# The adaLN products of a two-layer trunk: from VectorE and GpSimd to column strips on TensorE

## The chip, the cores and the metric

The kernel runs on one core of a Trainium2 chip. The metric is the device time of one execution in microseconds (us), lower is better. TensorE does the matrix products, VectorE, ScalarE and GpSimd work on tiles, and SyncE (SP) issues the loads. In the rows of the profile they are PE (with PEld for its weight loads), DVE, ACT, POOL and SP.

## The reference, cut to what matters

Two layers run over 512 tokens of width 1024. Each begins with an adaLN modulation: the conditioning vector `c` goes through SiLU and is multiplied by a 1024 x 6144 matrix, `w_ada`. The result is six vectors of 1024 (shift, scale and gate for each of two sub-layers).

```python
ada = jax.nn.silu(c) @ w_ada[l] + b_ada[l]      # 1 x 1024 times 1024 x 6144
# sub-layer 1: h = rms(x) * g_norm_mix * (1 + scale) + shift
# then w_in; branches GLA, DSA and RWKV-7; merge; w_out; gated residual
# sub-layer 2: the PEER mixer, with its own shift, scale and gate
```

The matrix is 24 MiB in fp32 for a layer and is read once. The product is a matrix with one vector, 6144 sums of 1024 terms. Shift and scale of sub-layer 1 (part 0 below) are needed before anything of the layer can be projected; the other parts are needed later.

## The kernel before, in words

Everything is fp32, and activations lie transposed: 128 partitions are 128 channels, `KD` = 8 tiles of channels by 512 tokens. Each engine has one instruction stream, written out in program order, and the streams meet on semaphores. Eight PSUM banks are handed out in the fixed order of `layer_banks()`: entry n takes bank n modulo 8 and waits until the entry eight places earlier has been read (`opened` on TensorE).

**Loads.** SyncE issues them in the order of `BLOCKS`, into a ring of two slots (`ring`; semaphores `landed`, `used`). The first three blocks, `("ada", 0..2)`, are 1024 x 512 pieces of `w_ada` of 2 MiB each. The other nine pieces come as 18 half blocks of 1024 x 256 (1 MiB) into two buffers `a_half`, between the blocks `rw` 1, 0 and 2 as `ADA_AFTER` says. Half block n waits for `ada_used[n % 2]`, so for the use of half block n - 2; SyncE issues in order, so a block behind a waiting half block waits too.

**The adaLN product.** In a loaded piece, partition p of tile k holds row 128 k + p of `w_ada`, and `cond[:, k]` holds SiLU(c) for the same rows. VectorE's `lane_sums` (L1251, L1254) multiplies tile k by the column `cond[:, k]` and adds the eight tiles up, lane by lane. VectorE does so for the three full blocks and for half blocks 0, 1, 3 and 17; GpSimd does it for the other 14 (L1731 multiplies all eight tiles, L1734 and L1736 add them in pairs). The result `a_at[block]` is 128 x 512: what is left is the sum over partitions. `adaln(part)` on TensorE (L468) takes it, with each 128 x 128 piece as the stationary side and a column of ones moving: 16 products of one column for each of three parts. `modulation(part)` on VectorE (L1277) adds the bias.

**The stage around it.** TensorE: sum of squares (L456), `adaln(0)`, then, once the normalized input `hT` is there, block `rw` 3 (tiles rp 12 and 13, L484), the products z and za (L496, L499), blocks `rw` 1 and `rw` 0 (four tiles each, L484), `adaln(1)`, the first tile of `rw` 2, the products kkn and bon (four each, L456), the other three tiles of `rw` 2, `adaln(2)`; then the RWKV steps (from L536). Each projected tile goes PSUM to ScalarE (L963) to VectorE, which mixes it with its shifted copy (L1309, L1311). After the fourth tile of `rw` 1, VectorE has a long piece of scans and elementwise products (L1347 to L1365). ScalarE then squares for kkn (L981), and VectorE makes the factors for bon (L1317). Before RWKV, VectorE needs the last tile (L1309, L1311) and four products with bon (L1371).

Of the kernel before, what the change touches and what calls it, by code (L numbers as in the profile page):

```python
# [20 lines left out]
P = 128  # L21
# [47 lines left out]
ADA_LENT = (3, 17)  # L69
# [45 lines left out]
def layer_banks():  # L115

    o = [("ss", 0), ("mod", 0)]
    o += [("rp", c) for c in (12, 13)] + [("z", c) for c in range(4)] + [("za", c) for c in range(4)]
    o += [("rp", c) for c in (4, 5, 6, 7, 0, 1, 2, 3)] + [("mod", 1), ("rp", 8)]
    o += [("kkn", c) for c in range(4)] + [("bon", c) for c in range(4)] + [("rp", c) for c in (9, 10, 11)] + [("mod", 2)]  # L120
# [35 lines left out]
def trunk(nc, fixed, cols, consts, x_t, w_ada, w_in, w_small, w_uq, w_iq, w_mac, w_mb, w_out, w_pq, uv, out,  # L156
          depth=L):
    ctx = ExitStack()
    with ctx:
# [19 lines left out]
        cond = sb("cond", KD)  # L179
        modc = sb("modc", 48)  # L180
# [128 lines left out]
        class Sig:  # L309
# [8 lines left out]
            ("squares", 1 + KD), ("h_ready", 2 * KD), ("cond_ready", 1), ("ada_summed", 6), ("ada_half_summed", ADA_HALVES - 4),  # L318
# [23 lines left out]
        const_set = sem("const_set")  # L342
        rstd_ready = sem("rstd_ready")
# [90 lines left out]
        def _(pe):  # L434
# [26 lines left out]
            for l in range(0, depth):  # L461
                def adaln(part):

                    ps = opened(("mod", part), l)
                    for j in range(16):
                        if part == 0 and j % 4 == 0:
                            need("ada_summed", l, j // 4 + 1)
                        last = mm(ps[:, 16 * part + j:16 * part + j + 1], a_at[4 * part + j // 4][:, j % 4 * P:(j % 4 + 1) * P], ones[:, 0:1],  # L468
                                  start=True, stop=True)
                    pe.drain().then_inc(B.filled(("mod", part)), 1)  # L470

                need("squares", l, 1)
                summed(("ss", 0), l, [(ones, hT[:, k, :]) for k in range(KD)])
                adaln(0)
# [3 lines left out]
                def block_of(name, l, jobs, width):  # L478

                    w = v3(arrive(name, l)[:, 0:8 * width], 8)  # L480
                    for i, (job, j, m) in enumerate(jobs):
# [1349 lines left out]
```

## Time and profile before

| | us |
|---|---|
| median of 3 runs | 5007.51 (5005.51 to 5007.78) |
| the profiled execution, its own time | 5002.27 |
| its span in the profile | 5000.5 |
| from the start to the first RWKV product, layer 0 | 231.56 |
| from the start of layer 1 (2494) to its first RWKV product (2711.25) | 217 |

The times are those of whole executions; every duration below is of the one profiled execution. "Span" is the time from its first to its last instruction, 1.8 us less than its own time. The two layers run the same program; the stage that the change touches lies at the start of each.

### The profile page before, as it was taken

The page shows a single profiled execution, that of the slowest core. Times are in us where ns is not written, and L with a number is a line of the kernel's source. Part 1 is how long each engine was busy: PE and PEld are TensorE (multiplying, and loading weights), DVE is VectorE, ACT ScalarE, POOL GpSimd, SP SyncE. Part 2 cuts the span into 40 slices and gives each one's busy share as a digit, 9 for nine tenths or more (in the row PEclk, how much of TensorE's full clock was granted, in tenths as well). Part 3 has the DMA queues.
Part 4 walks back from the last instruction along what each step waited for, and adds up shares of the span by engine and source line. Part 5 has one row for each costly group of instructions (what it writes and reads, how often), then busy time and mean ns, then how long its engine had stood idle before and what let it go on. Part 6 is the DMA issues. An engine that isn't in the chain of part 4 may idle for free.

```text
span 5000.5 us, 46222 instructions
## 1 busy us (share of the span) xinstructions
PE 4085.7 (82%) x12452; PEld 1976.0 (40%) x12452; DVE 2612.1 (52%) x5380; ACT 1478.2 (30%) x4170; POOL 2093.2 (42%) x2276
## 2 busy tenths in 40 slices
PE   5699999996777777787777999999877777877776
PEld 2387444553333233232234864454532332322222
DVE  6843235147656656654467422351566566566444
ACT  2121231213333333333312122221233333333333
POOL 4622000005666656666555210000066666666664
PEclk8899999998999899999978999999999989999999
DMA  6300111128999999999952001111299999999997
GB/s 225 109 1 1 43 63 64 59 74 345 404 386 393 388 391 392 392 402 415 385 198 76 1 1 56 56 59 59 101 372 404 381 397 383 397 401 387 403 409 316
DMA packets 223813, 1223.86 MB, mean 245 GB/s; under 512 B 18240, under 2 KB 59840, under 8 KB 89024
## 3 DMA queue, kind: packets, MB, share of 16 engines
q0 software_dynamic: 147456, 1073.81, 53.5%
q1 hardware_dynamic: 76096, 147.10, 8.4%
q8 instruction: 99, 1.62, 0.1%
q14 instruction: 162, 1.33, 0.1%
HBM read 1218.74 MB, written 2.10 MB: 244 GB/s over the span
## 4 chain that ended last, share of the span: by engine, by line
PE 25%; POOL 21%; issue 19%; DVE 13%; DMA 9%; PEld 5%; ACT 3%; DVEq 2%; PEldq 2%; POOLq 1%; ACTq 0%; SPq 0%
POOL reg L1777 14%; DMA reg<-uv,e_ic 7%; POOL e_ic L1774 7%; PE bank L888 4%; PE bank L567 3%; PE bank L456 3%; PEld bank L456 3%; PE bank L821 2%; PE bank L558 2%; DVE reg L1677 2%; DVE reg L1590 2%; DVE reg L1585 2%; PEld bank L749 1%; PE bank L649 1%; PE bank L630 1%
## 5 line engine op out<-in xcount | busy, mean ns | idle before, releaser
L888 PE MATMUL bank<-reg,hT 128*128 128x512 f32 x4096 | 2022.5, 637 | 616.7 <-ACT hT L1195 616.2
L1677 DVE CUSTOM_DVE_ANT_0 reg<-reg 128x1024 f32<-128x1024 f32 x1024 | 1256.4, 1227 | 1041.1 <-DMA reg<-uv,e_ic 963.7
L1777 POOL DMA_INDIRECT reg<-uv,e_ic x1024 | 1202.4, 1174 | 852.7 <-POOL e_ic L1774 757.8
L888 PEld LDWEIGHTS bank<-reg,hT 128*128 128x128 f32 x4096 | 773.0, 200 | 1863.6 <-ACT hT L1195 1103.8
L1774 POOL COPY e_ic<-e_idx 128x1 uint32<-128x1 uint32 x1024 | 496.3, 485 | 1462.6 <-DVEq L1655 1282.4
L1189 ACT ACTIVATE reg<-reg 128x1 f32<-128x1 f32 x1024 | 207.3, 202 | 1501.4 <-DVEq L1678 1501.4
L456 PE MATMUL bank<-hT,reg 128*128 128x512 f32 x1120 | 497.3, 598 | 8.2 <-issue 6.3
L1195 ACT ACTIVATE hT<-con,reg 128x128 f32<-128x128 f32 x1024 | 411.1, 401 | 72.3 <-issue 2.3
L456 PEld LDWEIGHTS bank<-hT,reg 128*128 128x128 f32 x1120 | 211.8, 191 | 283.6 <-issue 283.6
L1191 ACT ACTIVATE reg<-reg 128x1 f32<-128x1 f32 x1024 | 301.5, 294 | 71.7 <-issue 1.7
L1755 POOL TENSOR_TENSOR reg<-reg,con 128x512 f32<-128x512 f32 x112 | 140.8, 1270 | 392.7 <-ACTq L1014 223.1
L1528 DVE TENSOR_TENSOR reg<-bank,reg 128x512 f32<-128x512 f32 x48 | 33.2, 692 | 372.3 <-PE bank L749 216.6
L567 PE MATMUL bank<-reg 128*128 128x128 f32 x1408 | 179.8, 282 | 14.8 <-ACTq L1014 14.1
L567 PEld LDWEIGHTS bank<-reg 128*128 128x128 f32 x1408 | 164.8, 193 | 27.5 <-ACTq L1014 22.5
L749 PE MATMUL bank<-reg 128*128 128x512 f32 x384 | 172.6, 592 | 0.0
L484 PE MATMUL bank<-hT,reg 128*128 128x512 f32 x320 | 145.6, 617 | 24.0 <-ACT hT L955 23.5
L1731 POOL TENSOR_TENSOR reg<-reg,cond 128x2048 f32<-128x2048 f32 x28 | 107.0, 3821 | 137.8 <-DMA reg<-w_ada 129.9
L1114 ACT ACTIVATE reg<-bank 128x512 f32<-128x512 f32 x48 | 28.7, 597 | 458.6 <-PE bank L456 458.6
L558 PE MATMUL bank<-reg 128*128 128x128 f32 x768 | 110.4, 292 | 19.6 <-issue 16.6
L1734 POOL TENSOR_TENSOR reg<-reg 128x1024 f32<-128x1024 f32 (+1 forms) x56 | 116.8, 2085 | 15.2 <-issue 7.3
L1407 DVE TENSOR_TENSOR reg<-bank,reg 128x512 f32<-128x512 f32 x80 | 55.3, 691 | 124.7 <-PE bank L567 119.4
L1590 DVE FIND_INDEX8 reg<-reg 128x8 uint32<-128x128 f32 (+1 forms) x384 | 118.2, 329 | 0.0
(257 smaller groups left out, 3748.5 us busy)
## 6 DMA issues: line engine op xcount, KB each, us to landing
reg<-w_ada SPq DMA_DIRECT2D x36, 1024.0 KB, 5.2
reg<-w_mac SPq DMA_DIRECT2D x16, 1536.0 KB, 6.4
reg<-w_in SPq DMA_DIRECT2D x10, 2048.0 KB, 8.0
reg<-uv,e_ic POOLq DMA_INDIRECT x1024, 8.6
reg<-w_ada SPq DMA_DIRECT2D x6, 2048.0 KB, 12.1
reg<-w_mb SPq DMA_DIRECT2D x8, 1536.0 KB, 6.5
reg<-w_out SPq DMA_DIRECT2D x4, 2048.0 KB, 7.8
reg<-w_pq SPq DMA_DIRECT2D x4, 2048.0 KB, 7.8
```

The source lines that it names most:

```text
L456: last = mm(ps[:, 0:n], a, b, start=(i == 0), stop=(i == len(parts) - 1))
L558: last = mm(ps[:, i * P:(i + 1) * P], r_m[lv % 2][:, h, :], r_tn[:, h, :], start=True, stop=True)
L567: last = mm(ps[:, i * P:(i + 1) * P], a_[:, h, :], b_[:, h, :], start=True, stop=True)
L749: last = mm(ps[:, :], w[:, i, 8 + k, :], y[:, k, :], start=(k == 0), stop=(k == 3))
L888: last = mm(acc[j][:, :], e_diag[:, s_, :], e_row[s_][:, D + j * NB:D + (j + 1) * NB], start=False, stop=False)
L1189: A(e_ge[:, s_:s_ + 1], e_dot[:, s_:s_ + 1], ACT.Gelu)
L1191: A(e_wg[:, s_:s_ + 1], e_gc[:, s_:s_ + 1], ACT.Copy, scale=e_ge[:, s_:s_ + 1])
L1195: A(e_diag[:, s_, :], ident, ACT.Copy, scale=e_wg[:, s_:s_ + 1]).then_inc(diags[s_], 1)
L1590: V.max_index(places[:, g, 8 * r:8 * r + 8], vals[:, g, 8 * r:8 * r + 8], src[:, g, :])
L1677: V.tensor_tensor_reduce(e_row[s_][:, 0:D], e_row[s_][:, 0:D], e_hc, 1.0, 0.0, ALU.mult, ALU.add, e_dot[:, s_:s_ + 1])
L1774: pool.tensor_copy(e_ic[:, s_:s_ + 1], e_idx[:, bass.ds(t * SLOTS + g * GRP + s_, 1)]).then_inc(idx_ready, 1)
L1777: pool.indirect_dma_start(e_row[s_], None, uv, bass.IndirectOffsetOnAxis(ap=e_ic[:, s_:s_ + 1], axis=0))\
```

## The change

The lane sums go. (In the diff the `adaln_part` with `A(...)` is ScalarE's, the lines with `lane_sums` and `half_block` are VectorE's, those with `nc.gpsimd` GpSimd's, the rest TensorE's.) A loaded piece becomes the moving side of products on TensorE, and the stationary side is the conditioning vector: VectorE once copies `cond[:, k]` into 32 columns for each k (`condb`, 128 x 8 x 32). The product for tile k writes 32 partitions of a bank, the strip 32 (k % 4); all 32 rows of a strip are equal. Tiles k and k + 4 add up in one strip, so a piece takes 8 products and leaves four strips of partial sums. There are 21 pieces in a layer, `adaln_part(0..20)`: three of 512 columns, 18 of 256. ScalarE copies each bank to `a_at`, and `adaln(part)` works as before, but its moving column is now `sc[:, 4:5]`, which is 1 in rows 0, 32, 64 and 96 and 0 elsewhere.

Pieces 0 to 4 stand between the sum of squares and `adaln(0)`, 5 and 6 after block `rw` 3, 7 after z, 8 after za, 9 to 16 one behind each tile of `rw` 1 and `rw` 0, 17 and 18 after the first tile of `rw` 2, 19 and 20 between kkn and bon. The banks' order gets 21 entries more, each piece waits for its bank, and each ends with a drain of TensorE. The order of the loads stays; what frees their buffers is now TensorE. GpSimd does nothing ahead of the RWKV steps.

```diff
+                    need("ad_copied", l, (5, 13, 21)[part])
                     for j in range(16):
-                        if part == 0 and j % 4 == 0:
-                            need("ada_summed", l, j // 4 + 1)
-                        last = mm(ps[:, 16 * part + j:16 * part + j + 1], a_at[4 * part + j // 4][:, j % 4 * P:(j % 4 + 1) * P], ones[:, 0:1],
+                        last = mm(ps[:, 16 * part + j:16 * part + j + 1], a_at[4 * part + j // 4][:, j % 4 * P:(j % 4 + 1) * P], sc[:, 4:5],
...
+                def adaln_part(i):
+                    ps = opened(("ad", i), l)
+                    if i < ADA_RING:
+                        w, n, freed = v3(arrive(("ada", i), l)[:, 0:4096], 8), 512, used[block_at(("ada", i))[1]]
+                    else:
+                        h = i - ADA_RING
+                        pe.wait_ge(ada_landed[h % 2], 16 * (l * (ADA_HALVES // 2) + h // 2 + 1))
+                        w, n, freed = a_half[h % 2], 256, ada_used[h % 2]
+                    for k in range(KD):
+                        q = 32 * (k % 4)
+                        last = mm(ps[q:q + 32, 0:n], condb[:, k, :], w[:, k, :], start=(k < 4), stop=(k >= 4))
+                    last.then_inc(freed, 1)
+                    pe.drain().then_inc(B.filled(("ad", i)), 1)
...
-                need("ada_half_summed", l, 7)
-                need("ada_summed", l, 5)
                 adaln(1)
...
+                def adaln_part(i):
+                    ps = full(("ad", i), l)
+                    if i < ADA_RING:
+                        A(a_at[i], ps[:, :], ACT.Copy).then_inc(B.freed(("ad", i)), 1)
+                    else:
+                        h = i - ADA_RING
+                        A(a_at[ADA_RING + h // 2][:, h % 2 * 256:(h % 2 + 1) * 256], ps[:, 0:256], ACT.Copy).then_inc(B.freed(("ad", i)), 1)
+                    act.drain().then_inc(G["ad_copied"].sem, 1)
...
-                for i in range(ADA_RING):
...
-                    lane_sums(a_at[i], v3(dst[:, 0:4096], 8))
...
-                half_block(0)
-                half_block(1)
...
-                half_block(ADA_LENT[0])
...
-                        half_block(ADA_LENT[1])
...
-                for n in range(2, ADA_HALVES):
-                    if n in ADA_LENT:
-                        continue
...
-                    nc.gpsimd.tensor_tensor(w, w, bc(cond[:].unsqueeze(2), [P, 8, 256]), ALU.mult)
-                    pool.drain()
-                    for m in (4, 2):
-                        nc.gpsimd.tensor_tensor(w[:, 0:m, :], w[:, 0:m, :], w[:, m:2 * m, :], ALU.add)
-                        pool.drain()
-                    nc.gpsimd.tensor_tensor(a_at[block_i][:, n % 2 * 256:(n % 2 + 1) * 256], w[:, 0, :], w[:, 1, :], ALU.add)
```

TensorE, from the start of a layer to the products z. Before, the sum of squares (L456), `adaln(0)` (L468), the two tiles of `rw` 3 (L484) and the first z (L496):

```order
L456 MATMUL bank0<-hT,con 128x512 x8
L468 MATMUL bank1<-con,reg 128x1 x16
L484 MATMUL bank2<-hT,reg 128x512 x8
L484 MATMUL bank3<-hT,reg 128x512 x8
L496 MATMUL bank4<-reg,sw 128x512
```

And of the changed kernel, where L476 is a piece (its output form is that of one strip), L485 is `adaln`, L504 a tile of `rw` and L520 z:

```order
L459 MATMUL bank0<-hT,con 128x512 x8
L476 MATMUL bank1<-reg,condb 32x512 x8
L476 MATMUL bank2<-reg,condb 32x512 x8
L476 MATMUL bank3<-reg,condb 32x512 x8
L476 MATMUL bank4<-reg,condb 32x256 x8
L476 MATMUL bank5<-reg,condb 32x256 x8
L485 MATMUL bank6<-sc,reg 128x1 x16
L504 MATMUL bank7<-hT,reg 128x512 x8
L504 MATMUL bank0<-hT,reg 128x512 x8
L476 MATMUL bank1<-reg,condb 32x256 x8
L476 MATMUL bank2<-reg,condb 32x256 x8
L520 MATMUL bank3<-reg,sw 128x512
```

Five pieces now stand in front of `adaln(0)`, and two between `rw` 3 and z.

TensorE, from the last tile of `rw` 0 to the first kkn. Before:

```order
L484 MATMUL bank2<-hT,reg 128x512 x8
L484 MATMUL bank3<-hT,reg 128x512 x8
L468 MATMUL bank4<-con,reg 128x1 x16
L456 MATMUL bank5<-hT,reg 128x512 x8
L456 MATMUL bank6<-reg,con 128x512
```

And of the changed kernel, the same place, where L459 is first the tile of `rw` 2 and then kkn:

```order
L504 MATMUL bank1<-hT,reg 128x512 x8
L476 MATMUL bank2<-reg,condb 32x256 x8
L504 MATMUL bank3<-hT,reg 128x512 x8
L476 MATMUL bank4<-reg,condb 32x256 x8
L485 MATMUL bank5<-sc,reg 128x1 x16
L459 MATMUL bank6<-hT,reg 128x512 x8
L476 MATMUL bank7<-reg,condb 32x256 x8
L476 MATMUL bank0<-reg,condb 32x256 x8
L459 MATMUL bank1<-reg,con 128x512
```

Behind each projected tile stands a piece, and two more stand in front of kkn.

## Rows read from the trace of the kernel before

**Rows 1.** By stretch: length, busy us (instructions) of each engine, granted clock, DMA share, GB/s.

```profile
0.00:231.56 231.56, 143.68 (x369) 71.47 (x369) 173.72 (x141) 45.58 (x62) 127.82 (x60) 0.83 0.53 180
2494.00:2711.25 217.25, 151.62 (x369) 73.36 (x369) 162.71 (x135) 44.39 (x60) 125.88 (x56) 0.77 0.50 169
```

**Rows 2.** Timeline, TensorE, layer 0: start, us, what, xcount [idle before <-releaser].

```profile
116.51 27.70 PE L484 MATMUL bank<-hT,reg 128*128 128x512 f32 x64 [0.26 <-issue]
144.57 4.24 PE L468 MATMUL bank<-con,reg 128*128 128x1 f32 x32 [0.35 <-issue]
149.04 9.75 PE L456 MATMUL bank<-hT,reg 128*128 128x512 f32 x16 [0.23 <-issue]
171.88 5.16 PE L456 MATMUL bank<-reg,con 128*128 128x512 f32 x8 [13.08 <-ACT reg L981]
188.28 5.49 PE L456 MATMUL bank<-reg,con 128*128 128x512 f32 x8 [11.25 <-DVEq L1319]
193.61 20.76 PE L456 MATMUL bank<-hT,reg 128*128 128x512 f32 x48
224.37 6.96 PE L468 MATMUL bank<-con,reg 128*128 128x1 f32 x32 [9.99 <-DVEq L1342]
```

**Rows 3.** Timeline, TensorE, layer 1, at kkn, bon and `adaln(2)`.

```profile
2655.15 5.97 PE L456 MATMUL bank<-reg,con 128*128 128x512 f32 x8 [14.55 <-ACT reg L981]
2671.55 6.30 PE L456 MATMUL bank<-reg,con 128*128 128x512 f32 x8 [10.43 <-DVEq L1319]
2704.06 6.96 PE L468 MATMUL bank<-con,reg 128*128 128x1 f32 x32 [5.60 <-DVEq L1342]
```

**Rows 4.** Timeline, layer 0: VectorE, and GpSimd's last instruction of the stage.

```profile
119.78 11.47 DVE L1347 TENSOR_TENSOR_SCAN reg<-con,reg 128x512 f32<-128x512 f32 x4
165.13 3.93 DVE L1311 SCALAR_TENSOR_TENSOR reg<-reg,col 128x512 f32<-128x512 f32 x1
...
210.70 0.75 DVE L1311 SCALAR_TENSOR_TENSOR reg<-reg,col 128x512 f32<-128x512 f32 x1
...
215.45 2.29 DVE L1338 TENSOR_TENSOR reg<-reg 128x2048 f32<-128x2048 f32 x1
...
201.79 0.99 POOL L1736 TENSOR_TENSOR reg<-reg 128x256 f32<-128x256 f32 x1
```

**Rows 5.** Timeline at both layers' starts; last, the page's row of 2 MiB loads.

```profile
17.26 9.09 PE L456 MATMUL bank<-hT,con 128*128 128x512 f32 x16 [17.26 <-ACT hT L948]
...
53.04 12.30 DVE L1292 SCALAR_TENSOR_TENSOR hT<-xT,gain,rstd 128x512 f32<-128x512 f32 x8
...
66.15 15.42 PE L484 MATMUL bank<-hT,reg 128*128 128x512 f32 x32 [13.77 <-ACT hT L955]
...
2498.33 9.31 PE L456 MATMUL bank<-hT,con 128*128 128x512 f32 x16 [6.59 <-ACT hT L948]
...
2535.22 5.39 DVE L1292 SCALAR_TENSOR_TENSOR hT<-xT,gain,rstd 128x512 f32<-128x512 f32 x8
...
2541.42 16.81 PE L484 MATMUL bank<-hT,reg 128*128 128x512 f32 x32 [9.71 <-ACT hT L955]
...
reg<-w_in SPq DMA_DIRECT2D x10, 2048.0 KB, 8.0
```

**Rows 6.** Timeline, TensorE, a step whose products write two strips of 64 partitions.

```profile
276.66 0.34 PE L608 MATMUL bank<-reg 128*64 128x64 f32 x4
276.83 0.29 PE L609 MATMUL bank<-reg 128*64 128x64 f32 x4
276.94 0.34 PE L608 MATMUL bank<-reg 128*64 128x64 f32 x4
277.06 0.33 PE L609 MATMUL bank<-reg 128*64 128x64 f32 x4
```

**Rows 7.** By stretch, as rows 1: behind `adaln(1)` of layer 0.

```profile
149.00:151.00 2.00, 1.96 (x3) 0.96 (x4) 2.00 (x1) 0.00 (x0) 1.89 (x1) 0.50 0.00 0
```

More of the change, by code:

```diff
@@ L115, in layer_banks @@
 def layer_banks():
[L117 to L120, printed above, removed]
+    o = [("ss", 0)] + [("ad", i) for i in range(5)] + [("mod", 0)]
+    o += [("rp", 12), ("rp", 13), ("ad", 5), ("ad", 6)] + [("z", c) for c in range(4)] + [("ad", 7)] + [("za", c) for c in range(4)] + [("ad", 8)]
+    o += [x for i in range(4) for x in (("rp", 4 + i), ("ad", 9 + i))] + [x for i in range(4) for x in (("rp", i), ("ad", 13 + i))]
+    o += [("mod", 1), ("rp", 8), ("ad", 17), ("ad", 18)]
+    o += [("kkn", c) for c in range(4)] + [("ad", 19), ("ad", 20)] + [("bon", c) for c in range(4)] + [("rp", c) for c in (9, 10, 11)] + [("mod", 2)]
     for half, t, q, stage in rwkv_steps():
@@ L317, in trunk @@
         G = {n: Sig(n, k) for n, k in (
[L318 removed]
+            ("squares", 1 + KD), ("h_ready", 2 * KD), ("ad_copied", ADA_PARTS),
             ("pt_ready", 14), ("pt_used", 14), ("mixed", 14), ("lr_ready", 2), ("sig_ready", 2),
@@ L473, in _, with block_of @@
                 summed(("ss", 0), l, [(ones, hT[:, k, :]) for k in range(KD)])
+                pe.wait_ge(cond_spread, 1)
+                for i in range(5):
+                    adaln_part(i)
                 adaln(0)
                 need("h_ready", l, KD)
-                def block_of(name, l, jobs, width):
+                def block_of(name, l, jobs, width, parts=None):
                     w = v3(arrive(name, l)[:, 0:8 * width], 8)
@@ L951, in norm @@
                     inv_roots([(rstd[:], ("ss", w))], 1.0 / D, sc[:, 0:1], rstd_ready)
+                    if w == 0:
+                        for i in range(5):
+                            adaln_part(i)
                     for k in range(KD):
@@ L1241, in _ @@
             dve.wait_ge(loaded, 64)
+            V.tensor_tensor(sc[:, 4:5], ident[:, 0:1], ident[:, 32:33], ALU.add)
+            V.tensor_tensor(sc[:, 5:6], ident[:, 64:65], ident[:, 96:97], ALU.add)
+            dve.drain()
+            V.tensor_tensor(sc[:, 4:5], sc[:, 4:5], sc[:, 5:6], ALU.add)
+            dve.wait_ge(cond_ready, 1)
+            V.tensor_copy(condb, bc(cond[:].unsqueeze(2), [P, KD, 32]))
+            dve.drain().then_inc(cond_spread, 1)
             for l in range(0, depth):
@@ L1366, in _ @@
                         dve.drain()
-                need("ada_half_summed", l, ADA_HALVES - 5)
+                for i in range(2):
+                    dve.wait_ge(ada_used[i], (l + 1) * (ADA_HALVES // 2) + 1)
+                dve.sem_inc(passed, 1)
                 for c in range(4):
```

60 lines of the change are left out of this document (25 added, 35 removed).

## The prediction

> **What bounds the kernel now.** I first asked for each stretch how busy the engines were, then for the timeline of TensorE in the stage that the change touches. From the start to the first RWKV product TensorE works 143.7 of 231.6 us, and in layer 1 151.6 of 217 [rows 1]; VectorE is busier, 173.7 and 162.7. The rest of the span, 4550 us, does not run one changed instruction, so whatever happens comes from some 450 us. The timeline shows where TensorE stood still: 13.1 us ahead of kkn until ScalarE's square, 11.3 us ahead of bon, 10.0 us ahead of `adaln(2)` [rows 2], and the same three in layer 1, 14.6, 10.4 and 5.6 us [rows 3]. All end with something that VectorE made or set off. The reader is to see next why VectorE was late. The same instruction on the same form, L1311, took 3.93 us at 165.13 and 0.75 us at 210.70. GpSimd's last lane sum of the layer ended at 202.8, and behind it every VectorE instruction is at its short duration, 2.29 us for four times the size [rows 4]. So VectorE is slow while GpSimd runs its sums: the eight norm products of a layer took 12.3 us in layer 0, with GpSimd at work, and 5.4 us in layer 1, without [rows 5]. The last of the three stalls is another thing: VectorE's own sum of half block 17.
>
> **What goes.** VectorE's seven lane sums and GpSimd's 14 go in each layer. The long piece behind the fourth tile of `rw` 1 began at 119.78 and let the next tile be mixed some 40 us later. Its four scans took 11.47 us [rows 4]; undisturbed I estimate the piece at 18 to 22 us, from 2.29 us for each of its three products of 2048 columns and the shortest forms of the rest. VectorE would then be through at about 140, while TensorE is still projecting tiles until about 150. kkn waits for the first tile of `rw` 2 only, bon for nothing, and `adaln(2)` for no lane sum. I take away all three stalls in both layers: 13.1 + 11.3 + 10.0 + 14.6 + 10.4 + 5.6 = **65 us**. What is late next is TensorE itself.
>
> **Clock.** TensorE's granted clock was 0.50 (1.2 GHz) in the stretch behind the 32 one-column products of `adaln(1)` [rows 7], and it is low behind each stall. At full clock one of the two passes of a 512-column product takes 27.70 / 64 = 0.433 us [rows 2]. kkn and bon have 8 passes each, 3.6 us with the tail; they took 5.16, 5.49, 5.97 and 6.30, so **8.5 us** are to be had if no stall stands before them. `adaln(2)` took 6.96 us after its stall and 4.24 where the clock was still up [rows 2, 3]: **5.4 us** in two layers. Parts of the start of layer 1 ran slow after short waits that the pieces now fill; I put 3 us.
>
> **What is added on TensorE.** No row shows strips of 32. Upper bound for a piece of 256 columns: its 8 products in 16 passes run one after another, 16 x 0.217 = 3.5 us and the edges. Lower bound: four strips run at once, 4 x 0.217 = 0.87 us. The nearest row is the step that writes two strips of 64: 16 passes of 64 columns within 0.73 us of 276.66, the last one starting some 0.5 us after the first [rows 6]. Streaming alone would ask 0.433 / 8 = 0.054 us each, 0.87 us in sequence. And the second group of L608 is under way before the first L609 group is finished, though it stands behind it in the program. So strips do run beside one another, with two passes of each product waiting in their strip. I take the lower bound with edges: 0.26 us at the drain [rows 2] and about 0.16 us for the last pass to finish, 0.87 + 0.42 = **1.3 us**. A piece of 512 columns is 2.2 us at full clock, 3.9 at half.
>
> Part 3, section "The mechanism", of the page "TensorE: Matmul & The Clock Gate" of the Trainium skill says otherwise: products start and end strictly in program order, and a weight load overlaps a running product only in another row group. By that rule a strip's second pass would hold up the next strip, and the third rival below is what it gives. The L608 rows of this trace speak against it.
>
> From block `rw` 3 to RWKV 16 pieces stand on TensorE's path in each layer: 32 x 1.3 = **41.6 us**. Nothing hides them now that TensorE is the late one. Two small things more. Piece 7 needs half block 4, which is issued when piece 5 is done; between lie only piece 6 and z, about 4.7 us, and a half block takes 5 to 6, so 0.8 us a layer. And RWKV now waits for VectorE's last tile and bon products, about 5 us behind the last tile of `rw` 2, a little longer than `adaln(2)` covers: 0.8 a layer. Together **3.2 us**. ScalarE gets 21 copies of at most 0.6 us a layer; it is busy 45 of 231 us [rows 1], and only the last ones before `adaln(0)` stand on the path.
>
> **The start of a layer.** Before, lane sums ran beside the sum of squares. Now piece 0 waits for the end of that sum, 26.3 [rows 5], and frees its ring slot at 28.4, so block 2 is issued 4 us later. A 2 MiB load takes 8.0 us [rows 5]: it is there at 36.4. TensorE has been idle, so I put half clock: piece 2 to 40.3, pieces 3 and 4 to 44.7, the copy to 45.3, `adaln(0)` 5.6 us (between 4.24 and 6.96) to 50.9, the gain to 51.5. From there to `rw` 3 layer 1 took 6.2 us (2535.22 to 2541.42): 57.7 instead of 66.15, **8.4 us** less. Layer 1 by the same steps: 2507.6, 2509.8, 2517.8, 2521.7, 2526.1, 2532.3, then 0.7 to 2533.0, and 2539.2 instead of 2541.42, **2.2 us** less. That gain is mostly the norm products' 12.3 us in layer 0; the product itself ends no sooner.
>
> **Sum.** 65 + 8.5 + 5.4 + 3 + 8.4 + 2.2 = 92.5 us go, 41.6 + 3.2 = 44.8 come: 47.7 us less. The profiled execution would be 5002.3 - 47.7 = 4954.6; the median lay 5.2 above it, which gives 4960 (0.9902 of the time before). Following both layers' timelines step by step instead of adding terms I get 55 to 58 us, with some waits shrinking further; hence the lower end.
>
> **Rivals.**
> 1. *The strips overlap only in part* (reading four full-height strips at once may be slower than two). A piece then costs 1.7 to 2.0 us: 32 x 0.4 to 0.7 = 13 to 22 us, and 3 to 5 at the starts. Time 4976 to 4987. Nothing excludes it, since only two strips were ever seen.
> 2. *The clock stays down.* Behind the one-column products of `adaln(1)` the granted clock was 0.50 [rows 7] and the next tile took 9.75 us instead of 6.9 [rows 2], 2.9 us. Were that so behind each of the 13 places with pieces, 13 x 2.9 x 2 = 75 us come: -48 + 75 = 27 slower, 5035. It turns slower once more than 8 of the 13 places cost this. Against it: the pieces are short, and between most of them stand 6.9 us of full products.
> 3. *Strict order.* Each product's second pass waits for the first, and the next strip starts beside the second: 9 x 0.217 + 0.42 = 2.4 us a piece, 32 x 1.1 = 35 us; the starts lose 2.2 us at piece 0, 4.3 at piece 2, 4.3 at 3 and 4, 22 us in two layers. Time 4960 + 57 = 5017, at the edge of slower.
> 4. *No overlap at all.* 3.9 us a piece, 83 us more, and some 50 at the starts: about 5095.
> 5. *VectorE is not freed.* If GpSimd is not what slows it, only the 10.0 and 5.6 us stalls and its own sums go, and the pieces cost 41.6: about 5020. Against it: all of VectorE's rows before and after 202.8.
>
> **How the numbers follow.** The forecast has 0.66, rival 1 0.12, rival 2 0.07, rival 3 0.08, rival 4 0.04, rival 5 0.03. The bounds of the forecast itself are 4938 (the step-by-step reading, pieces of 1.2 us, higher clock) and 4975. To hold 8 in 10 the range takes in rival 1 and its tail: 4936 to 4998. A measurement of this kernel tells 0.2% from no change, 10 us. Faster by more: 0.66 + 0.12 + a part of rival 3, 0.80. Within: half of rivals 3 and 5, 0.08. Slower: rivals 2 and 4 and the rest, 0.12.
>
> **What would show it.** The pieces' line: a piece of 256 columns within 1.2 to 1.4 us, its 16 passes overlapping in time; 3.5 us would be rival 4, 2.0 us with each strip beginning at the second pass of the one before rival 3. VectorE's L1311 at 0.75 us throughout the stage, the long piece at 18 to 22 us. No stall of TensorE over 2 us between `rw` 1 and RWKV. The first RWKV product at about 205 instead of 231.6. Granted clock 1.00 between the tiles of `rw` 1 and `rw` 0. It is wrong if TensorE waits for half blocks (each wait ending with a load of `w_ada`), or if the RWKV steps or the PEER part, where nothing changes, move by more than 2 us.

## The result

The changed kernel took 4953.32 us (median of 4 runs, 4950.52 to 4969.54) against 5006.83 us for the kernel before (4 runs, 5005.51 to 5007.78): a ratio of **0.9911, interval 0.9893 to 0.9929**. It is faster, by 53.5 us; the forecast was 4960. The profiled execution took 4950.52, with a span of 4948.7 where the kernel before had 5000.5.

The stretches first (length; busy us and instructions of PE, PEld, DVE, ACT, POOL; granted clock; DMA share; GB/s): the stage of layer 0, what follows it up to layer 1, the stage of layer 1, and the rest. The first and third answer to [rows 1].

```profile
0.00:209.35 209.35, 167.41 (x705) 75.26 (x705) 61.82 (x89) 54.57 (x83) 0.20 (x4) 0.93 0.58 197
209.35:2471.60 2262.25, 1893.59 (x5850) 915.75 (x5850) 1135.35 (x2549) 689.98 (x2019) 921.45 (x1080) 0.95 0.64 253
2471.60:2663.86 192.26, 164.52 (x704) 73.98 (x705) 60.89 (x79) 52.99 (x81) 0.00 (x0) 0.92 0.55 188
2663.86:4948.70 2284.84, 1907.27 (x5866) 924.55 (x5866) 1140.49 (x2556) 698.37 (x2030) 920.12 (x1080) 0.94 0.63 251
```

The stage shrank from 231.56 to 209.35 and from 217.25 to 192.26 us, together **47.2 us**. The stretches behind were 2262.4 and 2289.2 us long in the kernel before and are 2262.3 and 2284.8 now; the 4.6 us there are scatter of the part behind, where nothing changed: its PEER mixer, from the first to the last gather of a layer, took 1355 to 1368 us over all the runs below. VectorE's busy time in the stage fell from 173.7 to 61.8 us, GpSimd's from 127.8 to 0.2, and TensorE's rose from 143.7 to 167.4.

TensorE in layer 0, timeline (start, us, what, xcount, [idle before <-releaser]), to be laid beside [rows 2]:

```profile
37.01 3.64 PE L476 MATMUL bank<-reg,condb 128*32 128x512 f32 x16 [6.26 <-DMA reg<-w_ada]
40.92 1.36 PE L476 MATMUL bank<-reg,condb 128*32 128x256 f32 x16 [0.28 <-issue]
44.31 3.70 PE L485 MATMUL bank<-sc,reg 128*128 128x1 f32 x32 [0.67 <-ACTq L976]
54.88 15.85 PE L504 MATMUL bank<-hT,reg 128*128 128x512 f32 x32 [6.87 <-ACT hT L992]
...
99.45 1.07 PE L476 MATMUL bank<-reg,condb 128*32 128x256 f32 x16
...
107.71 1.07 PE L476 MATMUL bank<-reg,condb 128*32 128x256 f32 x16
...
168.06 3.67 PE L459 MATMUL bank<-reg,con 128*128 128x512 f32 x8 [0.28 <-issue]
175.29 1.94 PE L476 MATMUL bank<-reg,condb 128*32 128x256 f32 x16 [2.36 <-DMA reg<-w_ada]
177.50 5.66 PE L459 MATMUL bank<-reg,con 128*128 128x512 f32 x8 [0.28 <-issue]
...
204.03 3.70 PE L485 MATMUL bank<-sc,reg 128*128 128x1 f32 x32 [0.26 <-issue]
209.35 3.47 PE L562 MATMUL bank<-reg 64*128 64x256 f32 x16 [1.62 <-DVE reg L1396]
```

A piece of 256 columns is 1.07 us. Two pieces between tiles start 8.26 us apart (99.45, 107.71), where the tiles of [rows 2] came every 27.70 / 4 = 6.93: a piece costs 1.33 us in place. kkn waits 0.28 us where it waited 13.08, `adaln(2)` 0.26 where it waited 9.99. Ahead of bon one wait is left, of another kind: piece 20 waits 2.36 us for half block 17, and with TensorE at rest the clock falls. The granted clock in three stretches there (pieces 17 and 18 for comparison, piece 20, bon; columns as above):

```profile
165.30:168.00 2.70, 2.18 (x33) 0.92 (x32) 1.44 (x2) 1.10 (x3) 0.00 (x0) 1.00 0.13 24
175.30:177.50 2.20, 1.92 (x16) 0.67 (x17) 1.68 (x3) 1.15 (x4) 0.00 (x0) 0.50 1.05 394
177.50:183.00 5.50, 5.50 (x8) 2.39 (x9) 0.00 (x0) 2.22 (x3) 0.00 (x0) 0.63 0.40 146
```

At 1.00 (2.4 GHz) a piece is 1.07 us and kkn 3.67; behind the wait, at 0.50 (1.2 GHz), the piece is 1.94, and bon 5.66. The wait cost 2.4 + 0.9 + 2.0 us in this execution, not 2.4. Layer 1 has the same (piece 20 stayed at full clock there), answering to [rows 3]:

```profile
2631.00 1.07 PE L476 MATMUL bank<-reg,condb 128*32 128x256 f32 x16 [2.54 <-DMA reg<-w_ada]
2632.35 5.33 PE L459 MATMUL bank<-reg,con 128*128 128x512 f32 x8 [0.28 <-issue]
2658.54 3.70 PE L485 MATMUL bank<-sc,reg 128*128 128x1 f32 x32 [0.26 <-issue]
```

VectorE, layer 0, its long piece (first and last rows), and all 28 instructions of the mixing line in one row (ns, min/median/max), answering to [rows 4]:

```profile
118.45 4.57 DVE L1368 TENSOR_TENSOR_SCAN reg<-con,reg 128x512 f32<-128x512 f32 x4
...
131.82 2.29 DVE L1386 TENSOR_TENSOR reg<-reg 128x2048 f32<-128x2048 f32 x1
```

```profile
L1335 DVE SCALAR_TENSOR_TENSOR reg<-reg,col x28: 750/752/753, 65.3 to 2659.8; 128x512 f32<-128x512 f32 x28
```

The scans take 4.57 us instead of 11.47, the long piece 15.7 us instead of 39.8, and no mixing instruction is above 753 ns. In the kernel before the same row reads:

```profile
L1311 DVE SCALAR_TENSOR_TENSOR reg<-reg,col x28: 751/1596/4026, 76.4 to 2704.8; 128x512 f32<-128x512 f32 x28
```

### The profile page after: what moved, and what is told of

Its sections match the earlier page's. It is cut to its first block, busy times and chain, and to the rows that moved or that the text cites. A ratio compares the mean times of both kernels' runs of the same rounds, so it can differ in the third digit from the quotient of the medians.

```text
span 4948.7 us, 47208 instructions
## 1 busy us (share of the span) xinstructions
PE 4132.8 (84%) x13124; PEld 1989.5 (40%) x13124; DVE 2398.6 (48%) x5272; ACT 1495.9 (30%) x4212; POOL 1841.8 (37%) x2164
## 4 chain that ended last, share of the span: by engine, by line
PE 31%; POOL 22%; issue 19%; DVE 9%; DMA 8%; PEld 4%; ACT 3%; DVEq 1%; PEldq 1%; POOLq 1%; ACTq 0%; SPq 0%
POOL reg L1781 15%; DMA reg<-uv,e_ic 7%; POOL e_ic L1778 7%; PE bank L914 5%; PE bank L459 5%; PE bank L593 3%; PE bank L504 3%; PEld bank L459 3%; PE bank L847 2%; PE bank L584 2%; DVE reg L1700 2%; DVE reg L1613 2%; PEld bank L775 1%; DVE reg L1608 1%; PE bank L675 1%
## 5 line engine op out<-in xcount | busy, mean ns | idle before, releaser
L459 PE MATMUL bank<-hT,reg 128*128 128x512 f32 x1120 | 497.1, 598 | 8.2 <-issue 6.2
L459 PEld LDWEIGHTS bank<-hT,reg 128*128 128x128 f32 x1120 | 211.9, 191 | 283.4 <-issue 283.4
L775 PE MATMUL bank<-reg 128*128 128x512 f32 x384 | 172.6, 592 | 0.0
L1159 ACT ACTIVATE reg<-bank 128x512 f32<-128x512 f32 x48 | 28.7, 597 | 458.6 <-PE bank L459 458.6
L504 PE MATMUL bank<-hT,reg 128*128 128x512 f32 x320 | 145.7, 610 | 16.7 <-ACT hT L992 13.7
L847 PE MATMUL bank<-reg 128*128 128x512 f32 x256 | 112.3, 593 | 3.5 <-DVEq L1555 3.5
L1058 ACT ACTIVATE reg<-bank 128x512 f32<-128x512 f32 x96 | 57.3, 597 | 182.7 <-PE bank L584 182.7
```

The source lines that it names most:

```text
L459: last = mm(ps[:, 0:n], a, b, start=(i == 0), stop=(i == len(parts) - 1))
L504: last = mm(ps[0:m, :], w[:, k, j:j + m], hT[:, k, :], start=(k == 0), stop=(k == KD - 1))
L775: last = mm(ps[:, :], w[:, i, 8 + k, :], y[:, k, :], start=(k == 0), stop=(k == 3))
L847: last = mm(ps[:, :], w[:, k, j * P:(j + 1) * P], m_o[:, k, :], start=(k == 0), stop=(k == KD - 1))
```

## Experiments

Times are medians; "before" was run beside them each time (4998.81, 4997.64 and 4996.51 us on three occasions, single runs from 4980 to 5014). Since most of that scatter comes from the PEER part, lengths of the stage are read from the profile beside the times: "R0" is start to first RWKV product in layer 0, "R1" the same from the start of layer 1. The kernel before has R0 231.6 and R1 217.2, the changed kernel 209.3 and 192.3. Each run has a label (x10, x8, ...), given with its result.

### The changed kernel once more

> The changed kernel itself once more, beside the two kernels below on one chip. The first run of it gave a ratio of 0.9911 to the kernel before, with stage lengths of 209.3 us (start to the first RWKV product, layer 0) and 192.3 us (layer 1). Expected: 4950 us (4940 to 4965), the same stage lengths within 2 us.

x10: 4955.84 us (4949.46 to 4968.22, 5 runs), ratio 0.9924 (0.9906 to 0.9941). R0 210.2, but R1 198.5: in this execution the start of layer 1 ran at a lower clock (the products of `adaln(0)` took 6.06 us, not 3.70) and waited longer for block 2 and for half block 4. So one profiled layer can be off by 6 us. A difference of stages below that needs both layers, or more than one run, to speak for it. The wait for half block 17 is there again, 3.36 and 2.54 us, but in layer 1 the clock did not fall behind it, and bon took 3.67 us:

```profile
2647.38 1.07 PE L476 MATMUL bank<-reg,condb 128*32 128x256 f32 x16 [2.54 <-DMA reg<-w_ada]
2648.76 3.67 PE L459 MATMUL bank<-reg,con 128*128 128x512 f32 x8 [0.31 <-issue]
```

The same wait therefore costs 2.5 us in one execution and 5.3 in another.

### Why was VectorE late? GpSimd's sums taken away from the kernel before

Edit, in the kernel *before*:

```diff
-                    nc.gpsimd.tensor_tensor(w, w, bc(cond[:].unsqueeze(2), [P, 8, 256]), ALU.mult)
-                    pool.drain()
-                    for m in (4, 2):
-                        nc.gpsimd.tensor_tensor(w[:, 0:m, :], w[:, 0:m, :], w[:, m:2 * m, :], ALU.add)
-                        pool.drain()
```

> The kernel before, with GpSimd's large multiplications and the first two additions of each half block left out (14 half blocks a layer; the adaLN vectors are then wrong for those): only its last addition of 256 columns stays. All else, VectorE's own sums too, is as before. Theory: this is the gain without its price on TensorE. The stalls ahead of kkn and bon go (13.1 + 11.3 + 14.6 + 10.4 = 49 us), the norm products of layer 0 are 7 us shorter, the stall ahead of adaln(2) stays; 50 to 60 us less, profiled time 4945 (4938 to 4955). Rival (VectorE's own sums and waits, not GpSimd, made it late): less than 15 us, above 4987.

x8: 4911.49 us (3 runs), ratio 0.9828 (0.9811 to 0.9845); R0 190.1, R1 176.5, together 82 us shorter than before. VectorE kept all its own sums. TensorE and VectorE in layer 0:

```profile
150.94 7.03 PE L456 MATMUL bank<-reg,con 128*128 128x512 f32 x16
182.99 6.87 PE L468 MATMUL bank<-con,reg 128*128 128x1 f32 x32 [4.42 <-DVEq L1342]
...
112.72 4.57 DVE L1347 TENSOR_TENSOR_SCAN reg<-con,reg 128x512 f32<-128x512 f32 x4
```

kkn and bon run as one group of 16 without a stall, at full clock, and the scans are back at 4.57 us. Only VectorE's own half block 17 is still late. I had expected 50 to 60 us. The 82 are the 49 of the two stalls, 9 at the layers' starts (`rw` 3 begins 6.4 and 2.9 us earlier), 7 off the stall ahead of `adaln(2)` (9.99 to 4.42 us in layer 0, 5.60 to 4.56 in layer 1), and 17 of clock, for which I had put nothing: kkn and bon together 9 us shorter, and 8 behind the start of `rw` 3 in layer 1. Against the changed kernel this one is 19.2 and 15.8 us of stage shorter, although it keeps that last stall: roughly the price of the pieces.

How deep VectorE's slowdown is follows from what GpSimd has running. In the kernel before, GpSimd's large product stood beside the slow L1311 of [rows 4], which ran from 165.13 to 169.06:

```profile
164.86 3.65 POOL L1731 TENSOR_TENSOR reg<-reg,cond 128x2048 f32<-128x2048 f32 x1 [0.35 <-issue]
```

It ended at 168.51, and L1311 0.55 us later. All 22 slow instructions of that line, of both layers, end 0.55 us after the GpSimd instruction that was running when they began, whether they took 1.06, 1.60, 2.68 or 3.93 to 4.03 us; the six with no GpSimd instruction beside them take 0.75.

### GpSimd kept busy in the changed kernel

Edit, in the changed kernel's GpSimd stream (110 in the first, 85 in the second; the product is not used):

```diff
+                pool.wait_ge(*B.full(("mod", 0), l))
+                pool.sem_inc(passed, 1)
+                scratch = e_idx[:].bitcast(F32)
+                for _ in range(110):
+                    nc.gpsimd.tensor_tensor(scratch, con[:, 0:512], con[:, 512:1024], ALU.mult)
+                    pool.drain()
```

> The changed kernel, with work put back on GpSimd that nothing uses: 110 products of 512 columns from two constant areas into a scratch area, in each layer, from the first adaLN part to shortly before the RWKV steps. Theory (VectorE was slow because GpSimd worked beside it): VectorE's L1335 goes back from 0.75 us to between 1.6 and 4, its long piece behind the fourth tile from 15.7 us to 35 to 40, and TensorE waits ahead of bon again; 12 us a layer, profiled time about 4975 (4965 to 4985) instead of 4950.5. Rival (VectorE was relieved only of its own sums): VectorE's durations and the time stay, 4950.

x1: 5005.95 us (9 runs), ratio 1.0019 (1.0002 to 1.0036): the whole gain was gone, 31 us more than I expected. R0 227.4, R1 204.3. The trace shows why the time overstates it:

```profile
51.66 184.77 POOL L1746 TENSOR_TENSOR e_idx<-con 128x512 f32<-128x512 f32 x110 [51.21 <-PEq L487]
227.42 3.84 PE L562 MATMUL bank<-reg 64*128 64x256 f32 x16 [7.28 <-DVE reg L1396]
237.99 1.11 PE L576 MATMUL bank<-con,reg 128*128 128x128 f32 x4 [5.93 <-POOL reg L1765]
```

The dummy products came 1.68 us apart, gaps included; one of them took 1.54 on average. They ran 9 us into the RWKV steps, held up GpSimd's first real product there, and slowed the steps (from the first product to the last y product 265 and 276 us, not 258 and 256). So I ran it with fewer.

> x1 with 85 idle products of 512 columns on GpSimd per layer instead of 110, so that they end before the RWKV steps begin (85 x 1.68 = 143 us from about 52 us on ends near 195 us). Theory (GpSimd's work beside VectorE's slows VectorE alone; it is this that made the stalls together with the sums): VectorE's 512-column products of the tile mixes take 1.6 us again instead of 0.75, the long piece about 31 us instead of 15.7, the stage is 5 to 15 us longer than the changed kernel's, and the RWKV steps behind it are as long as in the changed kernel (255 us, not 264 to 275 as in x1). Time 4970 (4955 to 4985). Rival (GpSimd's work does not matter, x1's loss came from its dummy work running into the RWKV steps): the stage stays at 209 and 192 us.

x1b: 4963.15 us (one run). R0 218.5, R1 196.4; the RWKV steps are back at 256 us in both layers, so x1's excess there was its overrun. GpSimd and VectorE in layer 0, then the norm products of layer 1; below, the mixing line:

```profile
48.62 137.77 POOL L1746 TENSOR_TENSOR e_idx<-con 128x512 f32<-128x512 f32 x85 [48.16 <-PEq L487]
50.06 13.47 DVE L1318 SCALAR_TENSOR_TENSOR hT<-xT,gain,rstd 128x512 f32<-128x512 f32 x8
128.91 8.51 DVE L1368 TENSOR_TENSOR_SCAN reg<-con,reg 128x512 f32<-128x512 f32 x4
...
2517.45 5.39 DVE L1318 SCALAR_TENSOR_TENSOR hT<-xT,gain,rstd 128x512 f32<-128x512 f32 x8
2524.62 5.48 POOL L1746 TENSOR_TENSOR e_idx<-con 128x512 f32<-128x512 f32 x4 [7.35 <-issue]
```

```profile
L1335 DVE SCALAR_TENSOR_TENSOR reg<-reg,col x28: 751/1598/1619, 75.1 to 2673.0; 128x512 f32<-128x512 f32 x28
```

GpSimd busy makes VectorE slow: 1.60 us for 0.75, and 13.47 for the eight norm products that take 5.39. Layer 1 holds its own control: GpSimd paused for 7.35 us there (why, no row shows), and the norm products in the pause took 5.39. The slowing goes both ways: GpSimd's dummies took 1.29 us each while VectorE waited (84 to 100 us) and 1.91 beside its scans. In layer 0 the norm, on which TensorE waits, pays 8 us. Behind the first product of `rw` 3 the stage is no longer than in the changed kernel there (154.1 us against 154.5), although the long piece took 31 us. Layer 1 is 2.0 us longer behind `rw` 3 (153.5 against 151.5), with waits for VectorE that the changed kernel has not, or has shorter:

```profile
2640.54 1.07 PE L476 MATMUL bank<-reg,condb 128*32 128x256 f32 x16 [1.44 <-DVE modc L1303]
2677.12 3.49 PE L562 MATMUL bank<-reg 64*128 64x256 f32 x14 [3.92 <-DVE reg L1396]
```

In x1, where the dummies ran on to the end, the wait ahead of RWKV was 7.28 and 9.17 us instead of 1.62. So the norm and the last tile are the main places where a slow VectorE is paid for.

**Why, then, are there no stalls of 11 to 15 us?** Not because VectorE has no sums of its own any more. In the kernel before, its lane sums lie outside the stretch that mattered: half block 3 ended at 74.6, after which VectorE stood waiting for tiles, and the next sum began at 219.86. Between them stands VectorE's work up to the factors of bon (L1317; L1341 in the changed kernel), here first the kernel before, then x1b:

```profile
65.68 8.95 DVE L1254 SCALAR_TENSOR_TENSOR reg<-reg,cond 128x256 f32<-128x256 f32 x7
178.76 9.44 DVE L1317 SCALAR_TENSOR_TENSOR reg<-reg,col 128x512 f32<-128x512 f32 x4
...
173.65 6.57 DVE L1341 SCALAR_TENSOR_TENSOR reg<-reg,col 128x512 f32<-128x512 f32 x4
```

And x8, which keeps all of VectorE's sums, has no stall ahead of kkn or bon. What differs is, first, the depth of the slowdown: from the scans to the end of the factors VectorE needed 68.4 us in the kernel before (119.78 to 188.2), beside GpSimd instructions of up to 5.26 us, and 51.3 in x1b, beside dummies of 1.25. Second, TensorE comes later by itself: it reaches kkn 112.4 us after the start of `rw` 3 in x1b, since it now has the pieces to do, and would have reached it after 92.6 in the kernel before. Which of the two counts for more no run here separates.

### What does a piece cost, and how far do strips overlap?

One strip and two strips instead of four, same products (ScalarE's copies and `adaln` then read 32 and 64 partitions); and four strips with the second product of a strip right behind its first:

```diff
-                        q = 32 * (k % 4)
-                        last = mm(ps[q:q + 32, 0:n], condb[:, k, :], w[:, k, :], start=(k < 4), stop=(k >= 4))
+                        last = mm(ps[0:32, 0:n], condb[:, k, :], w[:, k, :], start=(k == 0), stop=(k == KD - 1))
...
-                        last = mm(ps[q:q + 32, 0:n], condb[:, k, :], w[:, k, :], start=(k < 4), stop=(k >= 4))
+                        q = 32 * (k % 2)
+                        last = mm(ps[q:q + 32, 0:n], condb[:, k, :], w[:, k, :], start=(k < 2), stop=(k >= 6))
...
-                    for k in range(KD):
+                    for k in (0, 4, 1, 5, 2, 6, 3, 7):
                         q = 32 * (k % 4)
```

> The changed kernel with all eight products of a piece in one strip of 32 partitions, so 16 passes one after another. Theory (four strips at once): a piece of 256 columns takes 16 x 0.217 + 0.16 = 3.6 us instead of 1.07, 32 x 2.5 = 81 us more between rw 3 and RWKV and 20 to 25 a layer at the starts, time about 5075 (5050 to 5100), so slower than the kernel before. Rival (the strips never ran at once, the pieces are short for another reason): the piece and the time stay, 1.07 us and 4950.

> The changed kernel with the eight products of a piece in two strips instead of four. Theory: the time of a piece is its passes per strip, 8 x 0.217 + 0.16 = 1.9 us instead of 1.07; 32 x 0.83 = 27 us more, about 7 a layer at the starts, time about 4991 (4980 to 5000). Rival (beyond two strips something shared, such as reading, is the limit): 1.07 to 1.3 us, within 8 us of 4950.

> The changed kernel with the products of a piece in the order k = 0, 4, 1, 5, 2, 6, 3, 7: the four passes of a strip stand one behind another in the program. Theory A (TensorE looks past any number of passes that wait for their strip): 1.07 us and 4950, as before. Theory B (it looks past about three waiting passes, as many as the z products waited for before za began in the trace of the kernel before): the strips start one after another, 1.5 to 2.2 us a piece, 4970 to 5000. Rival (products start strictly in program order): four strips in sequence, 3.6 us, about 5075.

A piece of 256 columns in the trace of one strip, of two, and of four in the other order:

```profile
104.00 3.64 PE L475 MATMUL bank<-reg,condb 128*32 128x256 f32 x16
```

```profile
107.50 1.92 PE L476 MATMUL bank<-reg,condb 128*32 128x256 f32 x16
```

```profile
94.06 1.09 PE L476 MATMUL bank<-reg,condb 128*32 128x256 f32 x16
```

The runs are x2 (one strip), x3 (two) and x4 (the other order).

| strips | piece, us | R0 / R1 | time |
|---|---|---|---|
| one | 3.64 | 258.6 / 243.2 | 5043.06 (one run) |
| two | 1.92 | 220.0 / 208.4 | 4981.41 (one run) |
| four, second product of a strip right behind | 1.09 | 210.3 / 193.4 | 4950.54 (one run) |
| four, as changed | 1.07 | 209.3 / 192.3 | 4953.32 |

Everything follows 16 x 0.217 us divided by the number of strips, plus 0.2. With one strip the change is a loss, 44 us over before in that session; with two it keeps a third of its gain. The stages of one strip are 49 and 51 us longer than of four: 15 at each start, and 34 and 36 behind it, a little below 16 x 2.57 = 41, since longer pieces leave the half blocks time to land. The time came out 32 us below the 5075 expected: I had put 122 us on the stages and 100 came, and the part between the two stages was 9 us short in that one run. The fourth kernel is the sharp one for the mechanism. Strictly in program order, the second product of strip 0 would hold up the first of strip 1, and each strip would begin with the last pass of the one before: 13 x 0.217, about 3 us a piece. The order costs 0.02 us. So a product waiting on its own strip does not hold up one for another strip.

### The waits that are left

Half blocks 16 and 17 are used one tile of `rw` 2 later; and at the start of a layer the pieces stand in the order 0, sum of squares, 1, 3, 4, 2 (half blocks 0 and 1 are there before block 2). ScalarE and the order of banks follow.

```diff
+                values(1)
                 adaln_part(19)
...
-                for j in range(1, 4):
+                for j in range(2, 4):
...
+                pe.wait_ge(cond_spread, 1)
+                adaln_part(0)
                 need("squares", l, 1)
                 summed(("ss", 0), l, [(ones, hT[:, k, :]) for k in range(KD)])
-                pe.wait_ge(cond_spread, 1)
-                for i in range(5):
+                for i in (1, 3, 4, 2):
                     adaln_part(i)
```

> The changed kernel with the second tile of rw 2 moved ahead of pieces 19 and 20, so that half block 17 has 6.9 us more to land. Theory: TensorE's wait of 2.4 us for it goes, and the clock stays up, so that piece 20 takes 1.07 us and not 1.94 and the bon products 3.7 and not 5.7: 4 to 5 us a layer, time 4942 (4938 to 4946). Rival (VectorE's last tiles then set the start of RWKV): under 2 us a layer, 4947 to 4951.

x5: 4952.28 us (4 runs), ratio 0.9901 (0.9879 to 0.9922); R0 209.1, R1 202.9. In layer 0 the wait for half block 17 is gone and bon is back at full clock, and a part of the gain is given back some twenty microseconds on:

```profile
183.05 3.67 PE L459 MATMUL bank<-reg,con 128*128 128x512 f32 x8 [0.28 <-issue]
209.06 3.92 PE L563 MATMUL bank<-reg 64*128 64x256 f32 x16 [3.73 <-DVE reg L1397]
```

RWKV now waits 3.73 us for VectorE, where it waited 1.62. From `rw` 3 to RWKV 3.2 us are won (151.2 against 154.5), and the start before it was 3.0 us longer in this execution, so R0 is the same. Layer 1 was 11 us longer in that execution, with 7.8 us of waits for half blocks elsewhere, which is near the scatter of x10. The 4 to 5 us a layer that I expected did not come; by itself this move shows nothing that I could measure.

> The changed kernel with the pieces at a layer's start in the order 0, sum of squares, 1, 3, 4, 2. Block 2 is issued some 7 us earlier and lands 2 to 3 us earlier, and pieces 3 and 4 (3 us) lie in the wait for it. Theory: adaln(0) comes 5 to 6 us a layer earlier, time 4940 (4936 to 4944). Rival (the loads are the limit there, block 2 lands when it did): the 3 us alone, 4945.

x6: 4948.22 us (4 runs), ratio 0.9899; R0 204.2, R1 187.5. The start of layer 0:

```profile
18.53 3.64 PE L476 MATMUL bank<-reg,condb 128*32 128x512 f32 x16 [18.53 <-DMA reg<-w_ada]
35.38 1.92 PE L476 MATMUL bank<-reg,condb 128*32 128x512 f32 x16 [1.25 <-DMA reg<-w_ada]
50.84 9.51 PE L505 MATMUL bank<-hT,reg 128*128 128x512 f32 x15 [6.87 <-ACT hT L995]
```

Piece 0 frees its slot 6 us earlier, and the wait for block 2 falls from 6.26 to 1.25 us. `rw` 3 begins at 50.84 instead of 54.88, and in layer 1 5.9 us earlier after its start. The stages are 5.1 and 4.8 us shorter, so both layers agree with the theory's 5 to 6 about as well as the scatter lets one see; the time, 4948, lies above both forecasts. Block 2 came 1.6 and 2.5 us earlier, although its slot was free 6 and 9 us earlier.

> Both of the changes of order together (pieces 19 and 20 behind the second tile of rw 2; at the start 0, sum of squares, 1, 3, 4, 2). Theory: they add up, 9 to 11 us a layer, time about 4931 (4926 to 4938). Rival (the earlier start only moves a wait for a half block): 4938 to 4945.

> The changed kernel with both moves of order (pieces 0, sum of squares, 1, 3, 4, 2 at a layer's start; half blocks 16 and 17 after the last receptance tile) once more. Its profile before gave stages shorter by 7.3 and 6.5 us than the changed kernel's. If that is real: 4938 us, 12 to 15 us below the repeat of the changed kernel on the same chip. If it was only one execution's scatter, the two come out equal.

(The edit of both is the same; what the second text calls the last receptance tile is the second tile of `rw` 2.) First (x7) 4942.04 us (5 runs), ratio 0.9893 (0.9876 to 0.9910), then (x11) 4938.03 (4 runs), ratio 0.9892 (0.9874 to 0.9910); R0 202.0 and 202.3, R1 185.8 and 185.5. The stages repeat within 0.3 us. In its second session it lay 17.8 us below the repeat of the changed kernel; the two ratios' intervals still overlap a little (0.9874 to 0.9910, and 0.9906 to 0.9941), so the stages, 7 us shorter in each layer, are the better evidence. The 9 to 11 us a layer that I first expected did not come: 7.3 and 6.5. RWKV now waits for VectorE, 2.60 and 3.72 us in x11.

### A split that uses what was learned

If GpSimd made the trouble and not VectorE's own work, VectorE can take a part of the sums back, and TensorE is rid of that many pieces. Half blocks 2 to 9 go to VectorE, in its idle time between the mixes; the rest is x11's.

```diff
+                def half_block(n):
+                    dve.wait_ge(ada_landed[n % 2], 16 * (l * (ADA_HALVES // 2) + n // 2 + 1))
...
+                    V.tensor_scalar(out_, w[:, 0, :], cond[:, 0:1], None, ALU.mult)
+                    for k in range(1, KD):
+                        dve.drain()
+                        V.scalar_tensor_tensor(out=out_, in0=w[:, k, :], scalar=cond[:, k:k + 1], in1=out_, op0=ALU.mult, op1=ALU.add)
+                    dve.drain().then_inc(ada_used[n % 2], 1)
...
+                half_block(2)
+                half_block(3)
...
+                    for n in {0: (4,), 1: (5, 6), 2: (7,), 3: (8,), 4: (9,)}.get(i, ()):
+                        half_block(n)
```

> x11 with half blocks 2 to 9 given back to VectorE, which multiplies and adds them all by itself in its idle time between the tile mixes (8 products of 256 columns per half block, nothing on GpSimd); adaLN part 1 then takes the column of ones again. TensorE keeps pieces 0 to 4 and 13 to 20. Theory (the 32 small pieces per layer are paid in full on TensorE at 1.35 us each, and what cost the kernel before its time was GpSimd's share, not VectorE's): eight pieces fewer give 8 x 1.35 = 10.8 us a layer, 21 to 22 us over x11, so about 4918 us; the distance of two tile ends in the first half falls from 8.27 to 6.9 us, VectorE's half block takes 8 x 0.45 = 3.6 us in an idle slot of 6.8 us. Rival (VectorE's work again comes late, or hinders others): TensorE waits for the tile mixes, and less than 10 us is won. If the half blocks go one after another into the slots, VectorE is never the late one before adaLN part 1.

x9: **4911.85 us** (4902.79 to 4929.84, 5 runs), ratio **0.9844 (0.9822 to 0.9867)**: faster than both kernels, and than x11 in the same session. R0 187.4, R1 175.7, 14.9 and 9.8 us below x11, 24.7 where 21 to 22 were expected. (The 32 pieces of the expectation are those of both layers.) TensorE and VectorE in layer 0:

```profile
71.21 27.73 PE L510 MATMUL bank<-hT,reg 128*128 128x512 f32 x64
187.40 3.92 PE L565 MATMUL bank<-reg 64*128 64x256 f32 x16 [3.72 <-DVE reg L1414]
...
87.69 0.35 DVE L1330 TENSOR_SCALAR reg<-reg,cond 128x256 f32<-128x256 f32 x1 [0.25 <-issue]
88.11 3.84 DVE L1333 SCALAR_TENSOR_TENSOR reg<-reg,cond 128x256 f32<-128x256 f32 x7
92.78 0.69 DVE L1349 TENSOR_TENSOR reg<-reg 128x512 f32<-128x512 f32 x1 [0.83 <-ACTq L1006]
```

The four tiles of `rw` 1 follow each other in 27.73 us again, as in [rows 2]. VectorE takes 4.3 us for a half block and is back 0.8 us before the next tile. What bounds the stage's end now is VectorE's last tile and bon products (3.72 us).

## Why the prediction was right, point by point

- **The stalls (65 us): right.** All three go in both layers, and what came next was TensorE itself, as said. The reason named first, GpSimd's sums slowing VectorE, is the cause by x8, which alone gets 82 us of stage. Rival 5 falls. Two corrections. "VectorE is slow while GpSimd runs" does not by itself say that TensorE waits: in x1b VectorE is slow too, less deeply, and beside a later TensorE, and the two stalls are not there. And the reading that `adaln(2)`'s stall was VectorE's own affair holds for most of it only in layer 1: in x8, where half block 17 is still VectorE's, the stall shrinks from 9.99 to 4.42 us in layer 0 and from 5.60 to 4.56 in layer 1.
- **A piece, 1.3 us: right**, 1.07 and the gap, 1.33 in place. The lower bound, not the two-strip row, was what held; two strips measured 1.92. The argument from [rows 6], that a waiting pass does not hold up another strip's, is borne out by x4. Rivals 1, 3 and 4 fall. The page "TensorE: Matmul & The Clock Gate" of the Trainium skill (Part 3, section "The mechanism") has products start strictly in program order. This case's fp32 products in strips do not (x4: 1.09 us a piece), and the measurement decides.
- **Clock (13.9 + 3 us): right for kkn** (3.67 in both layers) **and `adaln(2)`** (3.70; the 4.24 forecast was the row of `adaln(1)`), **wrong for bon**, 5.66 and 5.33 instead of 3.6. The step that failed is "bon for nothing": I had given piece 7 a wait for its half block and none to piece 20, which stands just as near behind the piece that frees its buffer. SyncE issues half blocks 16 and 17 when pieces 17 and 18 are done, and a load of 2 MiB of `w_in` right behind (SyncE's row, both half blocks; then the page's row of all half blocks, whose median to landing was 5.2 us before):

```profile
166.54 1.72 SPq L422 DMA_DIRECT2D reg<-w_ada  x2
reg<-w_ada SPq DMA_DIRECT2D x36, 1024.0 KB, 6.7
```

  Half block 17 was issued at 167.89 and had landed at 175.29, 7.4 us later, with the stretch around it at 394 GB/s. TensorE wanted it at 172.93: between pieces 18 and 20 stand only kkn and piece 19, 5.2 us. That wait cost 5.3 us in layer 0 and 2.5 + 1.7 in layer 1, some 9.5 us that the sum lacks (4.9 and 2.5 in x10). It is also what the prediction had named as a sign of being wrong, a wait for a half block, and it is over the 2 us that no stall was to exceed. **The 3 us for the start of layer 1 were mis-sized**: before, layer 1 took 58.5 us from the first product of `rw` 3 to the first of `rw` 0 and layer 0 50.4; now the two agree within 0.5. So 8 us of clock came back there, not 3. Piece 7 waited 0.45 us and not at all, less than the 0.8 given; RWKV's wait for VectorE was 1.62, twice the 0.8.
- **The start of a layer (8.4 + 2.2): too small.** `rw` 3 began at 54.9 us (forecast 57.7) and 40.8 us into layer 1 (45.2): 11.3 and 6.6 us won. "The product itself ends no sooner" was wrong: `adaln(0)` ended 4.4 and 3.7 us sooner, and in layer 0 the norm gave the other 6.9. `adaln(0)` took 3.70 us and not 5.6, and pieces 3 and 4 ran at 1.36 and 1.07, not at half clock. I had taken TensorE to stay at half clock until `rw` 3; it was up again after piece 2. The repeat (6.07 and 6.06 us for `adaln(0)`) shows that this can go either way, so 7 of these us are partly luck of the profiled execution.
- **Sum.** 47.7 forecast, 47.2 measured in the stage. It fits better than its terms do, and that is luck: 9.5 us are missing for half block 17 and 1.6 for RWKV's wait, 7.3 were won at the starts and 5 of clock in layer 1 beyond the forecast. Behind `rw` 3, layer 0 gave 10.9 us where the terms add up to 18.2, and layer 1 18.4 where they add up to 19.0. The step-by-step reading, 55 to 58 us, was further off. One small term stands in no sum: z and za ran partly beside one another (both together 5.5 us before), and with piece 7 between them they take 3.67 and 3.69, 1.9 us more; pieces 5 and 6 cover the wait of 1.52 us for ScalarE ahead of z in return. Rival 2 did not come: between the tiles the clock is 1.00.
- **Figures that were wrong in themselves.** 4960 is 0.9905 of 5007.5, not 0.9902. Rival 5's terms give 5007.5 - 15.6 + 44.8 = 5037, not 5020, unless the rest that goes is worth 17 us, for which it names no row. Half of rivals 3 and 5 is 0.055, not 0.08. The last sign of being wrong, a part without changes that moves by more than 2 us, could not tell anything: the PEER parts moved by +3 and -9 us, within their scatter, and the RWKV steps by +2 and -3.
- The long piece took 15.7 us, below the 18 to 22 given.

## What to carry to other kernels

Where VectorE's durations for one form differ by a factor along the timeline, look at what GpSimd does then before moving VectorE's work: here silencing GpSimd was worth 82 us of stage, and VectorE could keep, even extend, its own part. The matrix-vector product with the vector as stationary side paid here only when spread over column strips: in one strip it lost 44 us, in four it won 41 to 54. And when a stall goes, the loads are asked for sooner; put each new consumer at least one load time behind the event that frees its buffer, since a 2.4 us wait cost 5.3 in one execution, with the clock that fell behind it.

## What the runs showed of the hardware

- fp32 products that write 32 partitions each run beside one another in four strips: 8 products of 256 columns take 3.64, 1.92 and 1.07 us in one, two and four strips. A product whose strip is busy does not hold up the next one for a free strip (1.09 against 1.07 us in the unfavourable order).
- GpSimd's elementwise products slow VectorE and are slowed by it. A VectorE product of 512 columns with two tiles as inputs took 0.75 us by itself, 1.60 beside 512-column products of GpSimd (x1, x1b), and up to 4.03 in the kernel before. There it ended 0.55 us after the GpSimd instruction beside which it began, in all 22 cases, so the longest GpSimd instruction (2048 columns, 3.6 us) cost the most. GpSimd's 512-column products went from 1.29 us to 1.91 beside VectorE's scans. I had expected the slowing of VectorE, not that GpSimd pays too.
- Behind a wait of TensorE of 2.4 to 2.5 us for a load the granted clock fell to 0.50 in both layers of the changed kernel, and did not in layer 1 of its repeat. One execution does not give the price of such a wait.
